# Strassen products for the up projections of a float32 transformer kernel, block sums on GpSimd

## What is computed

```python
def _swiglu(h, w_gate_up, w_down):                  # layers 1 and 2, D_FF = 2816
    gu = h @ w_gate_up
    gate, up = gu[..., :D_FF], gu[..., D_FF:]
    return (jax.nn.silu(gate) * up) @ w_down

def sqrelu_mlp(xn, w1, w2):                         # layers 3 and 4, 4096 hidden
    return jnp.square(jax.nn.relu(xn @ w1)) @ w2

# in each layer
h = h + mixer(rmsnorm(h, g_attn))
h = h + feed_forward(rmsnorm(h, g_ffn))             # rmsnorm: h / root(mean h^2 + eps) * g
```

## Time and profile before

| | before |
|---|---|
| median of three executions | 2266.15 us (2265.73 to 2266.15) |
| profiled execution, first to last instruction | 2264.0 us |
| PE busy | 2255.0 us, 100% |
| DVE busy | 1133.2 us, 50% |
| ACT busy | 898.8 us, 40% |
| POOL busy | 0.2 us |
| HBM read | 202.76 MB, 90 GB/s over the span |

### The profile page before, as it was taken

One profiled execution on the slowest core, in us unless ns is written; L12 is line 12 of the kernel. 1 busy time (PEld: TensorE's weight loads), 2 busy tenths in 40 slices (PEclk: granted clock), 3 DMA queues, 4 the chain that ended last, 5 costly groups with the idle time before them and its releaser, 6 DMA issues.

```text
span 2264.0 us, 26056 instructions
## 1 busy us (share of the span) xinstructions
PE 2255.0 (100%) x10682; PEld 1837.4 (81%) x10682; DVE 1133.2 (50%) x1756; ACT 898.8 (40%) x1419; POOL 0.2 (0%) x4
## 2 busy tenths in 40 slices
PE   9999999999999999999999999999999999999999
PEld 7677888888778888888889888888887767888887
DVE  5755443444575443345677754234445775432432
ACT  5654321223474322224534543123345885421331
POOL 0000000000000000000000000000000000000000
PEclk9999999999999999999999999999999999999999
DMA  4221222322222223222311222223322112222222
GB/s 156 82 78 70 98 95 96 106 93 87 91 99 75 93 82 114 94 88 93 117 63 65 83 103 93 93 93 100 106 100 75 56 56 77 102 101 93 93 94 93
DMA packets 36119, 206.54 MB, mean 91 GB/s; under 512 B 4128, under 2 KB 4640, under 8 KB 16672
## 3 DMA queue, kind: packets, MB, share of 16 engines
q1 hardware_dynamic: 33408, 199.17, 25.9%
q10 hardware_dynamic: 2592, 5.70, 0.8%
HBM read 202.76 MB, written 2.10 MB: 90 GB/s over the span
## 4 chain that ended last, share of the span: by engine, by line
PE 98%; DVE 1%; ACT 0%; issue 0%; ACTq 0%; DVEq 0%
PE ps L321 30%; PE ps L323 29%; PE ps L322 29%; PE ps L1159 2%; PE ps L2357 1%; PE ps L1214 1%; PE ps L1183 1%; PE ps L1890 1%; PE ps L1209 1%; PE ps L2376 1%; PE ps L1175 1%; PE ps L865 0%; PE ps L2367 0%; PE ps L1916 0%; PE ps L1919 0%
## 5 line engine op out<-in xcount | busy, mean ns | idle before, releaser
L321 PE MATMUL ps<-xh,high_w 128*128 128x512 f32 x1576 | 622.9, 395 | 0.0
L323 PE MATMUL ps<-xh,low_w 128*128 128x512 f32 x1576 | 614.1, 390 | 0.0
L322 PE MATMUL ps<-xl,high_w 128*128 128x512 f32 x1576 | 613.6, 389 | 0.0
L347 DVE TENSOR_TENSOR low_w<-raw_w,high_w 128x2048 fp32r<-128x2048 f32 (+3 forms) x203 | 420.0, 2070 | 168.6 <-ACT high_w L339 168.1
L339 ACT ACTIVATE high_w<-raw_w 128x2048 fp32r<-128x2048 f32 (+3 forms) x203 | 350.6, 1729 | 288.8 <-PE ps L323 281.5
L321 PEld LDWEIGHTS ps<-xh,high_w 128*128 128x128 f32 x1576 | 296.0, 188 | 63.7 <-issue 4.3
L323 PEld LDWEIGHTS ps<-xh,low_w 128*128 128x128 f32 x1576 | 295.8, 188 | 62.3
L322 PEld LDWEIGHTS ps<-xl,high_w 128*128 128x128 f32 x1576 | 296.2, 188 | 59.2 <-issue 0.2
L322 PE MATMUL ps<-ffn_hidl,high_w 128*128 128x512 f32 x864 | 336.1, 389 | 0.0
L323 PE MATMUL ps<-ffn_hidh,low_w 128*128 128x512 f32 x864 | 336.1, 389 | 0.0
L321 PE MATMUL ps<-ffn_hidh,high_w 128*128 128x512 f32 x864 | 336.1, 389 | 0.0
(11 more groups left out here) (307 smaller groups left out, 2438.4 us busy)
## 6 DMA issues: line engine op xcount, KB each, us to landing
raw_w<-in_w_f_gu SPq DMA_DIRECT2D x44, 1024.0 KB, 4.9
raw_w<-in_w_m_up SPq DMA_DIRECT2D x32, 1024.0 KB, 4.9
raw_w<-in_w_m_dn SPq DMA_DIRECT2D x32, 1024.0 KB, 5.0
raw_w<-in_w_f_dn SPq DMA_DIRECT2D x32, 704.0 KB, 4.1
raw_w<-in_w_b_qk SPq DMA_DIRECT2D x8, 1024.0 KB, 4.9
raw_w<-in_w_e_qk SPq DMA_DIRECT2D x4, 1024.0 KB, 5.9
raw_w<-in_w_e_out SPq DMA_DIRECT2D x4, 1024.0 KB, 5.6
raw_w<-in_w_o_q SPq DMA_DIRECT2D x8, 512.0 KB, 3.6
```

What stands on the lines that cost most here:

```text
L321: pe.matmul(out, sh, mh, start=start, stop=False)
L322: pe.matmul(out, sh, ml, start=False, stop=False)
L323: return pe.matmul(out, sl, mh, start=False, stop=stop)
L347: dve.tensor_tensor(wl[slot][:, 0:elems], raw[slot][:, 0:elems], wh[slot][:, 0:elems].bitcast(F32), ALU.subtract).then_inc(w_split, 1)
```

## The change

Each up projection is computed by Strassen's scheme in Winograd's form. The block is 2 x 2 in three directions: the chunk's two output tiles, the even and odd feature tiles, and two halves of 256 tokens. Four weight blocks (A11, A12, A21, A22; 128 x 512 each) and four activation blocks give seven products of 4 x 3 = 12 matmuls of 256 columns, 84 in a chunk, in place of 48 of 512 columns.

- GpSimd makes the four sums of weight blocks of a chunk: S3 and S1 in one add of 1024 elements a partition, S2 in one of 512, and one of 512 written over A21 (`sum_weights`). It waits for the load and, as the buffers are two, for the fourth product of the chunk before the last.
- ACT rounds the three sums (1536 elements) before the chunk's 2048, and DVE subtracts for both.
- Four sums of activation blocks are made once a layer, in the residual stage ahead of the norm (`forms_dve`, `forms_low`, and one ACT copy).
- ACT copies four partial results of 128 x 256 from PSUM to `kept` between the products (`keep`), since the later products go on adding in the same banks; DVE combines them.
- The first up chunk of each layer stays as it was (`plain`).
- The hidden width is cut in parts of 8, 7, 7 tiles (layers 1, 2) and 8, 8, 8, 8 (layers 3, 4). All down stages but the last of a layer have chunks of 256 output features (`nt = 2`, four chunks), the last one chunks of 128 (eight).
- The factor `rstd` is applied to the up part after the down projection: `resid_dve` multiplies by it before it adds. In layers 3 and 4 it is squared by the power -1.
- In an up stage DVE now splits chunk c+1 where it split chunk c+2. In the down stage the call with `c + 2` stays.

The diff, cut to its core:

```diff
-HALF_FF = FF // 2
-KF = HALF_FF // P
+FF_PARTS = (8, 7, 7)
 HID = 4096
+HID_PARTS = (8, 8, 8, 8)
+KH = 8
+HT = TOK // 2
...
+    def sum_weights(pool):
+        for c, f in FORM_OF.items():
+            slot = c % NS
+            w, to = four(raw[slot]), s_raw[f % 2]
+            pool.wait_ge(w_loaded[slot], 16 * (c // NS + 1))
+            if f >= 2:
+                pool.wait_ge(Z["product"], 6 * (f - 2) + 4)
...
+            pool.tensor_tensor(to[:, S3:S1 + 1, :], w[:, A11:A22 + 1:2, :],
+                               w[:, A21:A21 + 1, :].broadcast_to([P, 2, 512]), ALU.add).then_inc(Z["summed"], 1)
+            pool.wait_ge(Z["summed"], 3 * f + 1)
+            pool.tensor_tensor(to[:, S2, :], to[:, S1, :], w[:, A11, :], ALU.add).then_inc(Z["summed"], 1)
+            pool.wait_ge(Z["summed"], 3 * f + 2)
+            pool.tensor_tensor(w[:, A21, :], to[:, S2, :], w[:, A12, :], ALU.add).then_inc(Z["summed"], 1)

     def round_weights(act, upto):
         for c in range(prepared["act"], min(upto + 1, len(CHUNKS))):
             act.wait_ge(w_loaded[slot], 16 * (c // NS + 1))
+            if c in FORM_OF:
+                f = FORM_OF[c]
+                act.wait_ge(Z["summed"], 3 * f + 2)
+                act.activation(s_hi[f % 2][:, :, :], s_raw[f % 2][:, :, :], ACT.Copy).then_inc(Z["rounded"], 1)
+                act.wait_ge(Z["summed"], 3 * f + 3)
             act.activation(wh[slot][:, 0:elems], raw[slot][:, 0:elems], ACT.Copy).then_inc(w_rounded, 1)

     def split_weights(dve, upto):
+            if c in FORM_OF:
+                f = FORM_OF[c]
+                dve.wait_ge(Z["rounded"], f + 1)
+                dve.wait_ge(Z["summed"], 3 * f + 3)
+                dve.tensor_tensor(s_lo[f % 2][:, :, :], s_raw[f % 2][:, :, :], s_hi[f % 2][:, :, :].bitcast(F32),
+                                  ALU.subtract).then_inc(Z["split"], 1)
             dve.wait_ge(w_rounded, c + 1)
...
     def resid_dve(dve, R):
         def one(c, n):
             dve.wait_ge(w_used, c + 1)
+            if R.rooted:
+                wait_past(dve, R.added, n)
+                dve.tensor_tensor(xf[:, 0:R.nt, :], made, by, ALU.mult).then_inc(R.scaled.sem, 1)
+                wait_for(dve, R.scaled, n + 1)
+                made = xf[:, 0:R.nt, :]
+            dve.tensor_tensor(to, to, made, ALU.add).then_inc(R.added.sem, 1)
+            if forms:
+                forms_dve(dve, R.fold, n)
             if R.fold:
                 fold_dve(dve, R.fold, n)
+            if forms:
+                forms_low(dve, R.fold, n)
             split_weights(dve, c + 2)
...
+        def formed(c, n):                      # up_pe
+            pe.wait_ge(Z["split"], f + 1)
+            product(second, sums, S2, form(2), start=True).then_inc(Z["product"], 1)
+            pe.wait_ge(w_split, c + 1)
+            product(first, base, A11, half(0, 0), start=True).then_inc(Z["product"], 1)
+            product(third, sums, S3, form(1), start=True).then_inc(Z["product"], 1)
+            pe.wait_ge(Z["kept"], 4 * f + 1)
+            product(second, sums, S1, form(0)).then_inc(Z["product"], 1)
+            pe.wait_ge(Z["kept"], 4 * f + 2)
+            product(first, base, A12, half(1, 0)).then_inc(Z["product"], 1)
+            pe.wait_ge(Z["kept"], 4 * f + 3)
+            product(third, base, A22, form(3)).then_inc(Z["product"], 1)
+            pe.wait_ge(Z["kept"], 4 * f + 4)
+            product(second, base, A21, half(1, 1)).then_inc(w_used, 1)
...
+            elif U.swiglu:                     # up_act, a chunk
+                if n:
+                    silu(n - 1)
+                for which in range(4):
+                    keep(act, U, c, which)
+                if n:
+                    rounded(n - 1)
+                round_weights(act, c + 2)
...
+        def formed(c, n):                      # up_dve
+            split_weights(dve, c + 1)
+            if n:
+                made(n - 1)
...
```

More of the change, by code:

```diff
@@ L300, in sems @@
         return {n: sem(f"{tag}_{n}") for n in names.split()}
+    Z = sems("form", "summed rounded split product kept back top read")
     block = ctx.enter_context(nc.Block())
@@ L1604, in swa_kv_pe @@
                        k == 0, k == KD - 1)
[L1605 removed]
+        last.then_inc(kv_keys.sem, 1)
         root_pe(pe, f_attn1)
```

500 lines of the change are left out of this document (332 added, 168 removed).

## The result

The changed kernel takes 2430.53 us (2430.02 to 2431.72) against 2266.15: a ratio of 1.0726, 95% interval 1.0711 to 1.0741. It is slower, as forecast, but 74 us above the 2357 and 20 us beyond the range's end.

The account below looks back on a forecast made before the run. PE's matmuls were taken to bound the kernel, PE being busy 100% of the span. On the span of 2264.0: -57.6 + 63 + 21 + 2 + 62 = 2354.4; with 2.15 us from span to median, 2357 us, range 2285 to 2410.

Parts of the forecast that it names:

- Seven products for eight: Up stages: a formed chunk takes 10.08 us against 10.88; 72 such chunks gain 57.6 us.
- Handovers: From up to down stage, 14 times: PE waits for the second down chunk's late split, together 63 us.
- Layer starts: Start of each of four layers: PE waits for sums of squares and for kept products, 21 us in all.
- ahead of the sums of squares: Layer start: DVE's added work, 5.0 us against 2.4 spare, makes PE wait 2.6 us in each of four layers.
- for kept products: Layer start: ACT's 7.3 us before its first copy against PE's 4.3; waits of 3.0 us twice, 2.3 twice.
- GpSimd in the loop: Steady up chunks: GpSimd and DVE take turns, a chunk takes 11.5 us; 44 chunks lose 62 us, bounds 0 and 110.
- The rival in which they are hidden: Up chunks: GpSimd's adds end before 5.5 us, undelayed by DVE; chunks take 10.08, total 2295 us; chance 0.34 (2285 to 2310).
- One of the prediction's signs of being wrong: Up stages: the prediction is wrong if one of GpSimd's three adds takes more than twice DVE's time.
- a rival of 0.08: Whole kernel above 2410: worse contention, 2405 us; with PE at 1.2 GHz after pauses, 21 us more, 2426; chance 0.08.
- 2 for smaller ones: Output's last store and folds into next layers: one more multiplication (0.69 us) ahead of them, 2 us.

Follow-up runs that it names:

- fills: Changed kernel with GpSimd's three additions per formed chunk replaced by constant fills of the same regions, sums not computed: 2359.3 us, ratio 1.0413.
- The repair: Changed kernel with one line added: VectorE splits the second down chunk's weights at the end of the up part, in all 14 places: 2341.8 us, ratio 1.0332.
- the dummies: Changed kernel with 20 unread matmuls of 512 columns ahead of PE's wait at each second down chunk: 2408.8 us, ratio 1.0631.

## Why the forecast was right in sign and wrong in size

- **Seven products for eight, -57.6: right.** The chunk with fills took 10.08 us, as worked out.
- **Handovers, 63: right as a wait (62.2), short as a price.** The repair gave 88.7 us.
- **Layer starts, 21: measured 25.4, near by luck.** Its two parts missed in opposite directions: ahead of the sums of squares 10.4 were forecast and 23.2 measured (`xl` and `parts_sq`), for kept products 10.6 and 2.2. The forecast had DVE's work at its own speed; beside GpSimd it is stretched. With the fills both parts are nearly as worked out, 8.8 and 8.6. (Without the table load the prediction's own terms, 7.3 less 1.28 less 4.3, give 1.7 us and not its 2.3; the fills show 1.77.)
- **GpSimd in the loop, 62: right in kind.** Three additions last 5.3 us where GpSimd isn't held up, 4.8 was taken, and the steady chunk is 11.88, not 11.5. But 44 chunks were to lose 1.4 us each. In layers 1 and 2 it is 20 chunks that wait 1.5 us, three or four in a part where five were counted, and eight that wait 0.2 to 0.5; in layers 3 and 4 it is 12 that wait 0.6. Together 40 us (42.3 less 2.2). With layer starts and PE's slower restarts GpSimd's additions cost 71 us. The rival in which they are hidden (0.34) is refuted. One of the prediction's signs of being wrong came true: the addition of 1024 took 2.90 us on average, more than twice VectorE's 1.22.
- **Output projections: the first step that failed.** The prediction asked what DVE's new work delays at the layer's start, and not in the output chunks before it. PE ends the first two close together, and VectorE takes 15.9 us for both (from the addition at 202.54 to the split at 218.46) before it splits the fourth chunk's weights: 18.8 us that no term has.
- **The clock: the step that failed most.** The prediction put it into a rival of 0.08, "each microsecond that PE then worked at the 1.2 GHz level would cost a half. With 3 us at each of 14 handovers that makes 21". The sum itself took a wait to cost its own length. But the forecast's own 14 handovers, layer starts and chunk waits were some 150 us of pauses in a kernel that had none, and behind each pause of 2.6 to 5.9 us came a stretch at the lower level. Matmuls there cost 46 us more than at full clock. At the handovers the rival had the size right, 21 against 24; the dummies show it directly. It left out the other nine pauses of that length.

The waits that were forecast (148, with 2 for smaller ones) and those measured (151.5, with 5.0 of smaller ones) nearly agree by luck: the missed 18.8 offset the loop's 40 where 62 stood. What the sum lacks is the 46 us of clock and the 18 that come with the ends and restarts of the pauses. The steady chunk shows the latter, too: 11.88 less 10.08 less the wait of 1.54 leaves 0.26 us that no wait shows, 0.16 for the end and 0.10 for the restart.

## What to carry to other kernels

When PE is busy 100% of the time, price each new pause at its length and then again at the clock behind it: here 14 waits of 4.4 us on average cost 6.3 each, while those of 1.5 us cost 0.26 more than they show. When work is added to an in-order engine, list what stands behind it in every stage that the work is in, and repair the order before judging the arithmetic: a one-line move was worth 88.7 us, more than the whole scheme saves. Work put on GpSimd to relieve VectorE wasn't free here where VectorE had operations with two SBUF inputs, or scalings, at that time: 2.6 us of additions were cheaper on VectorE at 69% load than 6.6 us beside it.

## What the runs showed of the hardware

- Two-input additions on GpSimd of 128 x 1024 took 2.41 us, of 128 x 512 1.35; VectorE takes 1.22 and 0.69. The Trainium skill, "GPSIMD Engine Reference", section "Elementwise — side-by-side cycle accounting", has 4.5 us for 2048 elements, an estimated 2.25 for 1024: the trace is 7% above it.
- Fills on GpSimd of the same regions (0.96 and 0.53 us) left VectorE's two-input operations at their lengths, but not the scalings of 512 elements, with one input in SBUF: a pair takes 0.88 us, but 1.28 to 1.55 where it fell beside fills.
- At the layer's start VectorE's addition with PSUM as one input kept its length while GpSimd added (from 234.22), and the two scalings behind it, with one input in SBUF but at the faster rate of 0.44 each, were stretched from 0.88 to 2.99 (3.18, 3.11 and 3.23 in the other layers):

```profile
234.11 1.22 DVE L855 TENSOR_TENSOR h<-h,ps 128x1024 f32<-128x1024 f32 x1 [2.83 <-PE ps L347]
235.36 2.99 DVE L630 TENSOR_SCALAR scaled_xf<-h,gains 128x512 f32<-128x512 f32 x2
```

- Each of the changed kernel's 23 pauses of PE of 2.6 to 5.9 us was followed by matmuls at the lower clock, 0.427 us from start to start for 512 columns and 0.215 for 256, where full clock has 0.227 and 0.120. Behind the twenty waits of 1.5 us in the formed chunks there was none. With 20 matmuls in the pause none followed the 14 handovers; in that same kernel one did follow a pause of 1.88 us, so the length of a pause alone doesn't decide it.
